# Feed-forward run openings: the high parts of the combined activations one step later on ScalarE

## The reference, cut to what matters

```python
x = x + g1 * mix                                   # attention and convolution groups, then one projection
h2 = rms_norm(x, norm2_g) * (1 + sc2) + sh2
x = x + g2 * (jnp.square(jax.nn.relu(h2 @ w_ff1)) @ w_ff2)     # D = 1024, 4 D = 4096
```

## Time and profile before

| | us |
|---|---|
| median of 3 runs (lowest, highest) | 2680.43 (2674.95, 2681.03) |
| the profiled execution: time, span | 2682.67, 2680.8 |
| TensorE busy in the span | 2576.0 (96%) |
| VectorE, ScalarE, GpSimd busy | 1719.1, 1215.9, 1120.8 |
| openings 1, 2, 3 begin at | 1243.6, 1726.2, 2204 |

### The profile page before, as it was taken

How to read it: one execution, slowest core, us unless ns; L and a number is a source line. 1 busy time by engine, 2 the same in 40 slices (tenths; PEclk the granted TensorE clock), 3 DMA queues, 4 the chain that set the end, 5 groups by cost and what they waited for, 6 DMA issues and landing times.

```text
span 2680.8 us, 45790 instructions
## 1 busy us (share of the span) xinstructions
PE 2576.0 (96%) x16346; PEld 2282.1 (85%) x16346; DVE 1719.1 (64%) x3928; ACT 1215.9 (45%) x3051; POOL 1120.8 (42%) x770
## 2 busy tenths in 40 slices
PE   6999989998999889998899999999999999999998
PEld 3678867886777648886899999999999999999998
DVE  3258888998999557874655555555555555555555
ACT  3434323448888435654443333434433343444332
POOL 0000000007998025564554445545544453555553
PEclk7999999999999999998999999999999999999999
DMA  8757525844444975744234433442444244244222
GB/s 291 268 206 243 194 90 190 295 135 130 140 139 153 347 286 165 230 156 131 89 122 147 141 117 112 155 143 90 164 142 137 95 136 159 95 145 170 79 64 83
DMA packets 309615, 427.04 MB, mean 159 GB/s; under 512 B 23098, under 2 KB 238886, under 8 KB 302854
## 3 DMA queue, kind: packets, MB, share of 16 engines
q1 hardware_dynamic: 287514, 374.69, 41.9%
q0 software_dynamic: 4272, 39.19, 4.1%
q10 hardware_dynamic: 17604, 10.24, 1.3%
HBM read 351.63 MB, written 144.55 MB: 185 GB/s over the span
## 4 chain that ended last, share of the span: by engine, by line
PE 44%; issue 2%; DVE 2%; DMA 2%; POOL 1%; ACT 1%; SPq 1%; DVEq 0%; POOLq 0%; ACTq 0%
PE ff_u_ps L3222 15%; PE ff_u_ps L3224 15%; PE ff_u_ps L3223 15%; DMA gluT<-h_d 1%; POOL ff_w_lo L2867 1%; DMA out_y_prompt_dram<-ff_x_own 0%; DVE ff_wT L3079 0%; SPq L2785 0%; ACT ff_h_hi L2924 0%; ACT ff_w_hi L2915 0%; POOL ff_h_lo L2876 0%; DMA ff_x_own<-x_d 0%; PE ff_out_ps L3217 0%; DVE ff_x_own L3104 0%; SPq L258 0%
## 5 line engine op out<-in xcount | busy, mean ns | idle before, releaser
L2867 POOL TENSOR_TENSOR ff_w_lo<-gluT,ff_w_hi 128x512 fp32r<-128x512 f32 x342 | 458.1, 1347 | 410.6 <-ACT ff_w_hi L2915 410.6
L3222 PE MATMUL ff_u_ps<-ff_a_hi,ff_w_hi 128*128 128x352 f32 (+1 forms) x1536 | 493.7, 321 | 10.6 <-POOL ff_a_lo L2882 8.8
L3223 PE MATMUL ff_u_ps<-ff_a_lo,ff_w_hi 128*128 128x352 f32 (+1 forms) x1536 | 493.5, 321 | 0.0
L3224 PE MATMUL ff_u_ps<-ff_a_hi,ff_w_lo 128*128 128x352 f32 (+1 forms) x1536 | 493.4, 321 | 0.0
L3222 PE MATMUL ff_u_ps<-ff_h_hi,ff_w_hi 128*128 128x352 f32 (+1 forms) x1368 | 442.6, 324 | 13.3 <-DVE ff_h_lo L3027 5.4
L3224 PE MATMUL ff_u_ps<-ff_h_hi,ff_w_lo 128*128 128x352 f32 (+1 forms) x1368 | 440.0, 322 | 0.0
L3223 PE MATMUL ff_u_ps<-ff_h_lo,ff_w_hi 128*128 128x352 f32 (+1 forms) x1368 | 438.5, 321 | 0.0
L3122 DVE SCALAR_TENSOR_TENSOR ff_y<-ff_u_ps,modT,ff_y 128x352 f32<-128x352 f32 (+2 forms) x336 | 188.1, 570 | 316.7 <-PE ff_u_ps L3224 316.5
L2867 POOL TENSOR_TENSOR ff_w_lo<-ff_wT,ff_w_hi 128x512 fp32r<-128x512 f32 x168 | 225.5, 1345 | 272.5 <-ACT ff_w_hi L2915 172.9
L2915 ACT ACTIVATE ff_w_hi<-gluT 128x512 fp32r<-128x512 f32 x342 | 211.5, 626 | 275.9 <-PE ff_u_ps L3224 262.3
L3222 PEld LDWEIGHTS ff_u_ps<-ff_a_hi,ff_w_hi 128*128 128x128 f32 x1536 | 290.3, 189 | 12.6 <-POOL ff_a_lo L2882 10.0
(11 more groups left out here) (362 smaller groups left out, 4996.0 us busy)
## 6 DMA issues: line engine op xcount, KB each, us to landing
gluT<-in_w_ff_dram SPq DMA_DIRECT2D x192, 512.0 KB, 5.0
out_new_k_sample_dram<-in_cache_k_dram SPq DMA_DIRECT2D x40, 511.0 KB, 6.1
out_new_v_sample_dram<-in_cache_v_dram SPq DMA_DIRECT2D x40, 511.0 KB, 6.2
dwq<-in_w_ada_dram SPq DMA_DIRECT2D x32, 512.0 KB, 8.8
gluT<-in_cache_k_dram SPq DMA_DIRECT2D x16, 1024.0 KB, 9.2
gluT<-h_d SPq DMA_DIRECT2D x80, 176.0 KB, 5.1
mx_acc<-acc_d SPq DMA_DIRECT2D x16, 768.0 KB, 8.3
out_new_k_sample_dram<-in_cache_k_dram POOLq DMA_DIRECT2D x3, 4088.0 KB, 16.8
```

What stands on the lines that cost most here:

```text
L2867: pool.tensor_tensor(slot_view(w_lo, s), src, slot_view(w_hi, s).bitcast(F32), ALU.subtract).then_inc(w_lod, 1)
L3222: pe.matmul(out, w_hi[:, s % WR, w], hi, start=first, stop=False, skip_group_check=more)
L3223: pe.matmul(out, w_hi[:, s % WR, w], lo, start=False, stop=False, skip_group_check=more)
L3224: return pe.matmul(out, w_lo[:, s % WR, w], hi, start=False, stop=last, skip_group_check=more)
```

## The change

ScalarE's `s_high(run, k)` moves from the end of odd step 2k + 1 to the end of the next odd step. The last of the four goes behind the first down slot (k == 0), ahead of that slot's high part of weights. No instruction is added or taken away, and the queues of the other four engines are the same.

```diff
                                 if o % 2:
                                     a_high(e + o - 1)
                                     a_high(e + o)
-                                    s_high(run, 2 * j + o // 2)
+                                    if i >= 3:
+                                        s_high(run, 2 * j + o // 2 - 1)
                                 continue
...
                         for k in range(KT):
                             if blk == BLKS - 1 and run < NR - 1 and k < 4:
                                 h_high(run + 1, k)
+                            if blk == 0 and k == 0:
+                                s_high(run, 3)
                             if blk == 0 and k == 2:
                                 s1_high(run)
                             high(SLOT0[b] + up_slots(b) + k + WR)
```

## The result

The changed kernel takes 2693.32 us in the median of 4 runs (2690.07 to 2695.15), the kernel before 2678.8 (4 runs, 2674.95 to 2681.03): ratio 1.0059, 95% interval 1.0044 to 1.0074. Two later comparisons of the same pair gave 1.0049 (1.0037 to 1.0061) and 1.0049 (1.0033 to 1.0066). The change makes the kernel 0.5 to 0.6% slower, 13 to 16 us. The forecast was 2688.4 us, 0.30% slower.

A forecast was written before the change was run, and what follows sets the result against it. The stage is bound by TensorE's own work plus a few waits. Opening 1 -5.3, opening 2 +8.95 and opening 3 +4.3 make +8.0 us on the median 2680.43: 2688.4 us, 0.30% slower; range for 8 in 10, 2682 to 2696.

The forecast's parts named there:

- the clock in opening 1: Half clock behind TensorE's wait for low parts in opening 1 goes: -2.4 us.
- F4's start: Openings 2 and 3: F4 waits for an addition behind VectorE's late low parts of sum 0; +5.7 and +4.75 us.
- F6's wait: Openings 2 and 3: new wait for an addition behind the low parts of sum 1, 1.9 us in each.
- Low parts in openings 2 and 3: TensorE's waits for low parts of activations shrink to 0.4 us, gaining 1.2 and 1.5 us.
- Opening 1: Low part 4.0 us earlier, 2.4 us of clock regained, 1.1 us returned: -5.3 us (from -8 to -2).
- The 1.1 us that were to return as a wait for `y`: End of opening 1: sum 3 comes 1.1 us late for the next loads, costing 1.1 us.
- The thin cover: End of openings 2 and 3: six `s_high` cost nothing, 7.6 us against 7.6; if cover goes, up to 3 us return.
- rival (c): Openings' ends get late, loads held up: 3 us more in two or three openings, 2695 to 2697; 0.15 with (d).
- (a): Waits only, clock stays up at F4 and F6 of openings 2 and 3: +4.6, 2685.0 us; chance 0.15.
- (b): All openings gain, F4 and F6 find their additions done: 2668 to 2671 us; chance 0.05.
- (d): Opening 1 gives nothing, VectorE's chain slower beside GpSimd: +5 us on the sum, 2693; 0.15 together with rival (c).
- the clock in opening 3: At F4 the fall is there already, so 0 (-1.7 to +2); 0.85 us at F6; 1.7 regained at low parts.

The follow-up runs named there:

- r2: The changed kernel again, no edit, against the kernel before: ratio 1.0049 (1.0037 to 1.0061).
- r11: The changed kernel a third time, no edit, against the kernel before: ratio 1.0049 (1.0033 to 1.0066).
- r7: The changed kernel plus 36 unused matmuls on TensorE in front of F4 of openings 2 and 3; against the kernel before 1.0039 (1.0024 to 1.0055).
- r3: High parts of the sums one step later in opening 1 only, openings 2 and 3 in the old order; against the kernel before 0.9983 (0.9974 to 0.9992).
- r1: The kernel before, unchanged, against itself: ratio 0.9997 (0.9988 to 1.0005).
- r8: The kernel before with only the high parts of sums 2 and 3 one step later, in all openings: ratio 0.9976 (0.9965 to 0.9988).
- r6: The kernel before with VectorE's additions put between the four sums and their low parts, ScalarE in the old order: ratio 1.0011 (1.0000 to 1.0021).

## Why the prediction was right, and where its size was off

The mechanism was right where most of the cost lies: the waits at F4 and F6, and the way they come about through VectorE's queue. It was right for the low parts too. What did not come out is the clock in opening 1 and its size in openings 2 and 3. Of the listed signs, the waits for low parts were to fall under 3 us (3.5), and no half clock was to be left in opening 1 (1.6 us in the first trace). Sizes, measured against forecast:

- F4's start later by 5.5 us (opening 2; forecast 5.7) and 4.6 (opening 3; 4.75). The three low parts took 2.05 us; I had taken 2.1 between 1.40 and 3.22.
- F6's wait 2.0 us in both (forecast 1.9, though its own terms, 6.8 less 4.8, make 2.0).
- Low parts in openings 2 and 3: waits of 0.49 and 0.54 us (0.4).
- Opening 1: -4.9 us by the stretch S to A (485.3, mean of three, against 490.2, mean of two), -5.3 forecast. That the two are so near is partly luck, since errors of both signs cancel. The low part came 3.2 us earlier (41.4 us behind S in place of 44.6), not 4.0: on the scale of the kernel before at 1285.0, between the 1284.2 of the forecast and its late end of 1285.2. The wait left is 2.45 us, 2.1 to 2.5 in the three traces (forecast 1.7). Half clock was not gone behind it: 1.6 us in the first trace, 0 in r2, 1.7 in r11. The 1.1 us that were to return as a wait for `y` did not in the first trace (0.39 us; r11 0.43), and did in r2 (1.50 us against 0.56 before), where no clock fell.
- The end of openings 2 and 3: waits for `y` 0.58 and 0.93 us, against 0.45 and 0.78. The thin cover held; rival (c) did not come.

So the four rivals are out. The clock fell at both F4 in all three traces and at F6 in four of six places, and r7 ties it to the wait at F4 (a). F4 and F6 were not free (b), the loads behind the openings were not held up (c), and opening 1 did gain (d, r3). The time alone would have misled here: the 2693.32 us of the first comparison is the number of (d), 2693.

The term that was off most is the clock in opening 3. The forecast for opening 3 was +4.3 us; the stretch B to E grew by 6.0 (474.6 against 468.6). The step that was mis-sized is "in opening 3 the fall is there already, so nothing new (-1.7 to +2)", which rested on one trace. In the first trace of the kernel before the clock fell behind F4 (1.7 us); in r1 it did not, behind a wait of 1.97 us. So before has 0.85 us there in the mean of two traces. The changed kernel has 2.9, 1.4 and 2.8 us in its three, 2.4 in the mean: 1.5 us more, where the sum had 0. F6 of opening 3 lost clock in one trace of three, 0.6 us in the mean, where the sum had 0.85. With both, +4.3 becomes +5.5, and waits that came out 0.1 to 0.2 us longer make part of the rest. Opening 2 grew by 9.65 against 8.95; there the clock fell at F6 in all three traces (1.6 to 1.7 us, I had taken half of it), and at F4 it cost 1.7, 2.7 and 2.0 us (1.7).

By the traces the change costs 10.8 us (forecast 8.0), by the timed ratios 13 to 16. Two of the three intervals hold 10.8 (their lower ends are 12, 10 and 9 us), but all three centres lie above it, which is not explained. The timed executions have a mean granted clock each: 0.9805 over 15 of the changed kernel and 0.9829 over 76 of the kernel before. By this the changed kernel loses some 6 us more to the clock over the whole program, known to about 3 us; in the stage of the traces, idle time counted too, it is 4.3 us (14.1 against 9.8). That does not show that the timed executions lose more clock in the stage than the traced ones, nor rule it out, and the gap stays open.

## What to carry to other kernels

Before work is moved later on one engine, follow the other engines' queues from the instruction that waits for it: what stands behind that instruction, though it has nothing to do with it, becomes late too, and here it was the additions that TensorE's transposes need. The best version did not take the move back but put these additions ahead of the waiting instruction. With both edits the kernel gains 0.3 to 0.4%; with either alone and in full it gains nothing or loses. Moving only the sums that no transpose hangs on (r8) gains 0.24%. Price a fall of the clock by more than one trace, and check the parts of a sum and not only its total.

## What the runs showed of the hardware that was not expected

A wait of TensorE of about 2 us may or may not be followed by half clock, in the same kernel and at the same place. Behind F6 of opening 3 of the changed kernel the clock did not fall in the first trace (wait 1.99 us, shown above: its eight matmuls take 1.06 us) and did in r2:

```profile
2245.83 1.84 PE L3220 MATMUL ff_out_ps<-ident,ff_y 128*64 128x128 f32 x8 [2.00 <-DVE ff_x_own L3107]
```

```profile
2246.00:2247.00 1.00, 1.00 (x6) 0.50 0.38 152
```

At F4 of opening 3 of the kernel before it fell behind 1.89 us in the first trace and not behind 1.97 in r1:

```profile
2219.82 1.09 PE L3217 MATMUL ff_out_ps<-ident,ff_y 128*128 128x128 f32 x8 [1.97 <-DVE ff_x_own L3104]
```

```profile
2220.00:2221.00 1.00, 1.00 (x10) 1.00 1.05 370
```

Of the waits above 3 us in the openings (3.15 and 3.32 in r6, all others above 4) none was seen without a fall. The price of a fall is the busy time that it catches, and that differs with when it comes. Behind F4 of opening 3, with a wait of 6.51 us each time, it was 2.9 us in the first trace, where half clock lasted until near 2241, 5.8 us behind F4's start, and 1.4 in r2, where it ended near 2232.3, 2.8 us behind. Over the 13 traces a fall in the openings took 1.4 to 3.0 us of TensorE's time.
